# Hymba step on one core: another schedule of key products, cache rows and weight splits in the differential-attention stage

## The reference

```python
h  = rms_norm(x, norm_g)                       # x_prompt (1, 2048, 1024), x_sample (8, 1, 1024)
rq, rk, rv, rg, dq, dk, dv, dg = split(h @ w_in)      # 8 parts of 512 columns, 4 heads each
# group A: retention, 4 heads of 128, rotary, chunks of 128 positions, a state per head
# group B: differential attention, 4 heads; two 64-wide maps per head, 128-wide values
dq, dk = rope(rms_norm(dq, g_q)), rope(rms_norm(dk, g_k))
s = q . k * 64**-0.5 (causal);  p = softmax(s)
a = p[map 0] - lam * p[map 1];  o_diff = a @ dv
# sample rows: each of 8 rows attends to 4096 cached positions (32 pages of 128, picked by
# page_table) and to itself
u = concat(rms_norm(o_ret) * silu(rg), rms_norm(o_diff) * (1 - lam_init) * silu(dg))
y = x + u @ w_out
```

## Time and profile before

| | us |
|---|---|
| median of 3 runs | 1905.84 |
| lowest and highest run | 1899.58, 1907.33 |
| profiled execution | 1897.77 |
| its span, first to last instruction | 1895.9 |
| differential stage, slot 0 to the first matmul of the output stage | 715.3 to 1667.1 |

### The profile page before, as it was taken

One profiled execution on the slowest core, in us unless ns is written; L12 is line 12 of the kernel. 1 busy time (PEld: TensorE's weight loads), 2 busy tenths in 40 slices (PEclk: granted clock), 3 DMA queues, 4 the chain that ended last, 5 costly groups with the idle time before them and its releaser, 6 DMA issues. The chain is left out here.

```text
span 1895.9 us, 28473 instructions
## 1 busy us (share of the span) xinstructions
PE 1629.6 (86%) x8308; PEld 1203.4 (63%) x8308; DVE 1140.7 (60%) x1947; ACT 728.7 (38%) x1947; POOL 1040.1 (55%) x1927
## 2 busy tenths in 40 slices
PE   6869789898778977898999988998987975589999
PEld 1247657576565745676877766776766863366886
DVE  2569577676676633777766879665786753124521
ACT  2333232232132222555655655665554654210000
POOL 4648576767566634787546878556578643200000
PEclk9989999899899988999999999999998997689999
DMA  8752676656647632322015222223223013144441
GB/s 290 265 175 88 196 217 194 214 151 186 216 147 223 191 115 67 90 67 78 23 55 164 80 78 78 68 84 101 79 90 117 29 56 122 56 149 150 145 133 57
DMA packets 169627, 240.99 MB, mean 127 GB/s; under 512 B 15393, under 2 KB 82090, under 8 KB 169458
## 3 DMA queue, kind: packets, MB, share of 16 engines
q1 hardware_dynamic: 164082, 222.33, 37.7%
q0 software_dynamic: 3072, 8.43, 1.1%
q10 hardware_dynamic: 2320, 8.42, 1.1%
HBM read 211.37 MB, written 27.76 MB: 126 GB/s over the span
## 5 line engine op out<-in xcount | busy, mean ns | idle before, releaser
L589 POOL TENSOR_TENSOR s_ring<-s_ring,s_q_row 128x1024 f32<-128x1024 f32 x128 | 317.4, 2496 | 59.9 <-DMA s_ring<-in_cache_k 56.6
L1607 PE MATMUL s_z<-g_w_hi,s_h_hi 128*128 128x512 f32 x512 | 225.0, 439 | 24.7 <-DVE s_h_lo L1502 14.3
L1065 PE MATMUL s_z<-g_w_hi,s_h_hi 128*128 128x512 f32 x512 | 229.1, 448 | 19.0 <-DVE s_h_lo L964 16.8
L1067 PE MATMUL s_z<-g_w_hi,s_h_lo 128*128 128x512 f32 x512 | 207.6, 405 | 0.0
L1066 PE MATMUL s_z<-g_w_lo,s_h_hi 128*128 128x512 f32 x512 | 206.8, 404 | 0.0
L1609 PE MATMUL s_z<-g_w_hi,s_h_lo 128*128 128x512 f32 x512 | 205.2, 401 | 0.0
L1608 PE MATMUL s_z<-g_w_lo,s_h_hi 128*128 128x512 f32 x512 | 204.6, 400 | 0.0
L1351 ACT ACTIVATE s_p<-s_sc,s_neg_max 128x1024 f32<-128x1024 f32 (+4 forms) x192 | 166.8, 873 | 76.4 <-DVE s_neg_max L1532 50.7
L1656 PE MATMUL s_o<-s_v,s_aT 128*128 128x128 f32 x1088 | 167.0, 296 | 14.8 <-ACT s_aT L1332 14.7
L1656 PEld LDWEIGHTS s_o<-s_v,s_aT 128*128 128x128 f32 x1088 | 145.2, 202 | 52.2 <-ACT s_aT L1332 48.9
L964 DVE TENSOR_TENSOR s_h_lo<-g_hT,s_h_hi 128x512 fp32r<-128x512 f32 x128 | 165.0, 1328 | 8.7 <-ACT s_h_hi L861 5.0
(11 more groups left out here) (241 smaller groups left out, 3552.8 us busy)
## 6 DMA issues: line engine op xcount, KB each, us to landing
s_ring<-in_cache_k SPq DMA_DIRECT2D x256, 256.0 KB, 2.9
s_ring<-in_cache_v SPq DMA_DIRECT2D x256, 256.0 KB, 2.8
w_raw<-in_w_in SPq DMA_DIRECT2D x8, 2048.0 KB, 10.3
s_w_raw<-in_w_in SPq DMA_DIRECT2D x56, 256.0 KB, 4.4
x_in<-in_x_prompt SPq DMA_DIRECT2D x16, 512.0 KB, 6.9
s_table<-c_rope_ret SPq DMA_DIRECT2D x64, 128.0 KB, 3.2
u_scratch<-s_gate POOLq DMA_DIRECT2D x32, 256.0 KB, 2.6
s_u_in<-u_scratch SPq DMA_DIRECT2D x16, 512.0 KB, 4.9
```

What stands on the lines that cost most here:

```text
L589: pool.tensor_tensor(slot[:], slot[:], bc(R.q_row[:].unsqueeze(1), [P, 2, 512]), ALU.mult).then_inc(R.keys_times_q, 1)
L1065: pe.matmul(b[:], hi[:, c, :], g.w_hi[:, wc, :], start=(wc == 0), stop=False)
L1067: last = pe.matmul(b[:], lo[:, c, :], g.w_hi[:, wc, :], start=False, stop=(wc == DC - 1))
L1607: pe.matmul(z_bank[:], hi[:, c, :], g.w_hi[:, wc, :], start=(wc == 0), stop=False)
```

## The change

- `DIFF_PLAN`: the keys of rows 5, 6, 7 stand in slots 1 to 12, 14 to 26 and 28 to 39 (before 3 to 14, 28 to 36, 50 to 58), the values in 18 to 25, 33 to 40 and 48 to 55 (before 20 to 27, 42 to 49, 64 to 68).
- GpSimd: `finish` goes ahead of the key products and one slot later. A slot's key products wait for `qk_low`, VectorE's `split_qk` of that slot; where a slot has three, the first waits for `combine` instead.
- VectorE: in "light" slots (at most two groups of four key blocks in tile c, which is t = 5 to 12, and slots without c) the sums over keys stand behind `split_qk` instead of at the slot's head.
- ScalarE: of the eight high parts of a head's weights four stand early in slot t = 15 and four at the head of the next slot; those of the output weights stand at the head of a slot, and are spread 4, 3, 3, 3, 3 over slots 64 to 68 (before 4, 4, 4, 4 over 64 to 67).

```diff
-def row_keys_pool(pool, R, s):
-    for r, j in R.keys.get(s, []):
+def row_keys_pool(pool, R, s, part=slice(None)):
+    for r, j in R.keys.get(s, [])[part]:
...
 DIFF_PLAN = [
-    (list(range(3, 15)), 14, list(range(20, 28))),
-    ([28, 29, 30, 32, 33, 34, 35, 36], 36, list(range(42, 50))),
-    (list(range(50, 59)), 58, list(range(64, 69))),
+    ([1, 1, 2, 2, 3, 3, 4, 5, 6, 7, 8, 9, 10, 11, 12, 12], 12, list(range(18, 26))),
+    ([14, 14, 16, 16, 17, 17, 17, 18, 19, 20, 21, 22, 23, 24, 25, 26], 27, list(range(33, 41))),
+    ([28, 28, 29, 29, 29, 30, 30, 32, 32, 33, 34, 35, 36, 37, 38, 39], 42, list(range(48, 56))),
 ]
...
         def out_weights_at(s):
-            first = 4 * (s - TILES)
-            return range(first, first + 4) if 0 <= first < 2 * DC else range(0)
+            x = s - TILES
+            return range(0) if not 0 <= x < 5 else range(4) if x == 0 else range(3 * x + 1, 3 * x + 4)
...
                 if is_block(c - 1):
                     square_output(c - 1, s)
+                if 1 <= k < NH and t == 0:
+                    for x in range(DC // 2, DC):
+                        split_w(k, x)
+                for x in out_weights_at(s):
+                    split_out_weights(x)
                 if is_block(a + 1):
                     split_qk(a + 1)
                 if s + 1 < TILES:
                     split_h(2 * s + 2)
+                if border:
+                    for x in range(DC // 2):
+                        split_w(k + 1, x)
...
-                if border:
-                    for x in range(DC // 2):
-                        split_w(k + 1, x)
...
-                if border:
-                    for x in range(DC // 2, DC):
-                        split_w(k + 1, x)
...
-                for x in out_weights_at(s):
-                    split_out_weights(x)
                 row_exp_act(act, R, s)
...
-            for s in range(SLOTS + 1):
+            for s in range(SLOTS + 2):
...
-                row_keys_pool(pool, R, s)
...
+                done = s - OLAG - 3
+                if is_block(done) and done % GROUP == GROUP - 1:
+                    finish(done // GROUP)
+                a, c = s - SLAG, s - OLAG
+                if len(R.keys.get(s, [])) >= 3:
+                    pool.wait_ge(combined, FIRST_COMB[c] + 1)
+                    row_keys_pool(pool, R, s, slice(0, 1))
+                    pool.wait_ge(qk_low, a + 2)
+                    row_keys_pool(pool, R, s, slice(1, None))
+                else:
+                    if is_block(a + 1) and s in R.keys:
+                        pool.wait_ge(qk_low, a + 2)
+                    row_keys_pool(pool, R, s)
...
-                if is_block(s - OLAG - 2) and (s - OLAG - 2) % GROUP == GROUP - 1:
-                    finish((s - OLAG - 2) // GROUP)
...
-                row_keys_dve(dve, R, s - 1)
+                light = not is_block(c) or len(groups_of(c % NT)) <= 2
+                if not light:
+                    row_keys_dve(dve, R, s - 1)
...
                 if is_block(a + 1):
                     split_qk(a + 1)
+                if light:
+                    row_keys_dve(dve, R, s - 1)
                 if s < TILES:
                     gate_z(s)
```

## The result

The changed kernel takes 1941.7 us (median of 4 runs, 1939.71 to 1945.84) against 1902.7 for the kernel before beside it: ratio 1.0204, 95% interval 1.0175 to 1.0232. It is 39 slower. The forecast was 1912, its own range 1897 to 1927, the wide one 1880 to 1942, which holds the result by 0.3. The profiled execution took 1939.71 (before 1897.77), so 42 are to be found in the trace.

A forecast was written before the change was run, and what follows sets the result against it. TensorE was taken to bound the kernel, so the differential stage's time adds straight to the total. Gains of -82.0 and light-slot losses of +88.2 give +6.2, a median of 1912; own range 1897 to 1927, wide range 1880 to 1942.

The forecast's parts named there:

- Ring chain in light slots: Slots 21 to 25, 37 to 40: TensorE waits for value pieces behind the key; +67.5 chain, +20.7 clock, together +88.2.
- Slots 5 to 15 at -10.8: Slots 5 to 15 take 121.2 for 132.0: 114.6 bare plus 11 keys at 0.6 each.
- slots 26 to 31 at +0.3: Slots 26 to 31 take 76.5 for 76.2: 71.7 plus 8 keys at 0.6 each.
- A key at 0.6: Each key piece, its product behind `split_qk`, adds 0.6 us to a slot; bounds 0 and 1.3.
- Slot 16's pile of 10.4: GpSimd, slot 16: two key products (10.4) behind four remainders and `norm_and_rope`, ending 6 to 7 into slot 17.
- 5.2 for one product in the way: Slots 32 to 36: one key product in the way adds 5.2, within 87.5 for 90.9.
- Borders: Slot 16 loses about 6.7 of its 23.2 through early high parts; slots 16 to 20 together come to +4.
- Drain: The drain, up to the output stage, takes some 92 for 134.1: -42, bounds -29 and -55.
- 48 to 63: Slots 48 to 52 take 80.2 for 91.6, -11.4; slots 53 to 63 take 116.9 for 131.9, -15.0.
- that TensorE does not wait for pieces: Rival: in light slots SP's wait ends early, so only the gains stay, 1824; chance 0.10.
- That the clock costs nothing: Rival: the light slots' chain forms, but the clock costs 0 to 6 instead of +20.7, 1892; chance 0.30.
- The slower rival: Rival: the lower clock lasts through each light slot, costing 4.1 instead of 2.3, 16 more, 1928; chance 0.22.

The follow-up runs named there:

- e1: Changed kernel with the two value pieces ahead of the key piece in each slot's ring order: 1872.4 us, ratio 0.9841.
- e3: Changed kernel with the sums over keys at the head of every slot, as before the change: 1879.0 us, ratio 0.9876.
- e10: Changed kernel with 24 unused matmuls ahead of the value pieces in slots 21 to 25 and 37 to 40: 1927.1 us, ratio 1.0108.
- e6: e1 with GpSimd's weight remainders at a border waiting for VectorE's split_qk of that slot: 1855.0 us, ratio 0.9734.
- e12: Changed kernel with the border's eight high parts back where they were before (both fours late in slot t = 15): 1934.5 us, ratio 1.0154.
- e5: Kernel before with the changed plan of rows alone: 1894.9 us, ratio 0.9958.
- e13: Changed kernel with the output weights' high parts back at the slot's end, 4, 4, 4, 4 over slots 64 to 67: 1954.2 us, ratio 1.0270.
- e4: Changed kernel with the earlier plan of rows (two row ends one slot later) and the output weights' high parts as before: 1887.9 us, ratio 0.9916.
- e9: e1 without GpSimd's waits for qk_low and combined ahead of the key products: 1880.1 us, ratio 0.9876.
- two halves: e4, everything but the plan and the output weights (ratio 0.9916), and e5, the plan alone (0.9958).

## Why the prediction was right or wrong

- *The whole*: the wide range held by 0.3 us, and that is luck. The prediction let 1942 be reached only by the lower clock throughout, a key at 1.3 and a drain of -25; the runs show 9 for the clock, 0.8 a key and -35.7, and the missing time is the heavy slots' below. The point forecast of +6 lies within what the prediction called the same; slower, which came, had 0.39 of the chances.
- *Bound and structure*: right. TensorE sets the pace of the stage, and what its slots gain or lose adds up to the total (42.1 in the table, 42 measured).
- *Ring chain in light slots*: right in mechanism and total (+87.6 for +88.2), shown by e1, e3 and the timeline. That the total is right to 0.6 is luck, since the two parts were mis-sized against each other: by e10 the clock is worth about 9 (at least, since it rose to 0.95 only), not 20.7, and what is left for the chain is nearly 79 (87.6 less 8 to 9), not 67.5. In slot 22 the place comes free at +7.7 (7.0 taken), and the last piece lands 7.9 later, as predicted.
- *Slots 5 to 15 at -10.8*: wrong, +4.3; *slots 26 to 31 at +0.3*: wrong, +13.1. This is the step that failed: "114.6 + 11 keys x 0.6" and "71.7 + 8 x 0.6" price a key by what it does beside VectorE once the products stand behind `split_qk`, and forget where its product ends. Held back, the product runs into the next slot and beside its splits (26.5 for 24.7 in slots 5 to 15, where I had 0.8 a split). In even slots it also stands behind `norm_and_rope`, and the head of a heavy next slot waits for it: slot 13 is 18.9 (12.1 with the sums last), slot 29 is 18.3 (13.0 before). I counted this wait at slots 17 and 33 alone, though the same rows applied. And slots 15 and 31 take 21.2 and 21.9 where e6 has 14.6 and 15.1, because brought-forward high parts free remainders beside the combine. Measured against these runs, the four slots hold 25 of the 28.
- *A key at 0.6*: slots 5 to 12 take 83.0; the same t without keys, slots 53 to 60 less three value pairs, 75.5; nine keys, so 0.8. Right enough. But I read 5.20 as one product; the row's count is two, and one takes 2.4. That entered two terms. Slot 16's pile of 10.4 should have been 5, without harm, since the pile ended even later than I put it, 8.4 into slot 17. The "5.2 for one product in the way" in slots 32 to 36 is the length of two; that this stretch came out at -3.4 to the tenth is luck.
- *Borders*: the gain of 7 came (23.2 to 16.4), but e12 shows that it was given back in slots 15 and 17. In the sum for 16 to 20, +4 for +3.1, this was right; the price at slot 15 was missing.
- *Drain*: -35.7 for -42; my slots of 15 were a little short. Its bound of -29 was misread: the eight matmuls of 1.14 are those of a pair of pieces, so 16 pieces take 9 and not 18, and the bound is -20. Of the 51 gained from slot 53 on, e5 and e13 give 38 or 39 to the plan and 12 or 13 to the new places of the output weights. *48 to 63*: right within 1.
- *Rivals*: that TensorE does not wait for pieces fell with the first row. That the clock costs nothing (0 to 6) fell with e10, but its 8 to 9 lies nearer to that rival than to my 20.7. The slower rival had the right side and nearly the size, but not the cause: the lower clock cost less than I took, and the missing time came from the heavy slots.

## What to carry to other kernels

In a ring that is filled in program order, a piece whose place is freed late in a slot must not stand ahead of pieces that are needed in that slot; swapping the two was worth 69 here, with the same transfers and products in the same slots. A consumer at a slot's head is only safe if its producer's whole queue, in every parity of the slot, ends in the slot before. And a weight split moved earlier on one engine moves its partner on another: look at what two-input VectorE work then stands beside it.

## What the hardware showed that I had not expected

- A combine of 128 x 384 that takes 0.61 alone took 6.00 beside four GpSimd remainders of 1.25 to 1.28 each, which is what they take without it. Twelve such records in seven kernels (the changed one, e1, e3, e4, e9, e10, e13) take 5.96 to 6.05, start 0.6 to 0.7 ahead of the first remainder and end 0.4 behind the last. So it was held for all four, not slowed by a share, though its record starts first. Where it started in the middle of a remainder (e4 and e9, once each) it took 1.63 and the remainders beside it 1.73 and 1.60, so the moment at which it starts matters.
- Filling TensorE's waits of 4 to 10 us with unused matmuls raised the granted clock from 0.79 to 0.95 and made the kernel faster, 1927.1 for 1941.7 (10.9 between the profiled executions).
- The kernel's two halves, each faster than before (0.9916 and 0.9958), are slower together (1.0204).
